# Experts' loop: the first high half of the next up weights moved ahead of ScalarE's evacuation of the block's output

## The reference, cut to what matters

```python
def run_block(args):
    tok, e = args
    xb = hf[jnp.minimum(tok, n_tok - 1)]
    a = xb @ w_gate[e]          # 128x1024 @ 1024x512
    b = xb @ w_up[e]            # 128x1024 @ 1024x512
    return (jax.nn.silu(a) * b) @ w_down[e]   # 128x512 @ 512x1024
```

## Time and profile before

| what | value |
|---|---|
| time, median of 3 runs | 2508.34 us (2498.53 to 2517.55) |
| the profiled execution, its own time | 2503.58 us |
| its span in the trace | 2502.0 us |
| granted TensorE clock over the span | 0.992 |
| 33 blocks of the experts' loop, first evacuation 548.14 to 1146.77 us | 598.63 us, 18.14 us each |
| weights of one expert | 3 x 2048 KB |

### The profile page before, as it was taken

How to read it: one execution, slowest core, us unless ns; L and a number is a source line. 1 busy time by engine, 2 the same in 40 slices (tenths; PEclk the granted TensorE clock), 3 DMA queues, 4 the chain that set the end, 5 groups by cost and what they waited for, 6 DMA issues and landing times. The chain is left out here.

```text
span 2502.0 us, 33881 instructions
## 1 busy us (share of the span) xinstructions
PE 2411.4 (96%) x11969; PEld 1979.1 (79%) x11969; DVE 1910.0 (76%) x2471; ACT 1352.4 (54%) x1914; POOL 589.0 (24%) x492
## 2 busy tenths in 40 slices
PE   7999999999999999999889999999999999999999
PEld 3766678668888888886789999997788888788887
DVE  5876668678988989897877888887776666657786
ACT  3243323257777787775676676676434434444332
POOL 2000354143333232333611110110043333300000
PEclk9999999999999999999999999999999999999999
DMA  7778356589878899998521111113333433587864
GB/s 268 223 240 294 106 197 217 227 309 397 337 272 308 306 403 404 409 398 339 175 68 52 51 51 52 51 39 134 111 110 105 161 139 139 197 305 259 301 253 152
DMA packets 181315, 535.36 MB, mean 214 GB/s; under 512 B 17710, under 2 KB 77714, under 8 KB 167880
## 3 DMA queue, kind: packets, MB, share of 16 engines
q1 hardware_dynamic: 163900, 470.20, 51.5%
q0 software_dynamic: 12592, 45.63, 4.8%
q10 hardware_dynamic: 4700, 17.92, 1.8%
HBM read 443.38 MB, written 90.33 MB: 213 GB/s over the span
## 5 line engine op out<-in xcount | busy, mean ns | idle before, releaser
L1756 PE MATMUL psum<-w_high,block_hT_high 128*128 128x512 f32 x576 | 232.3, 403 | 4.0 <-DVE w_low L1374 2.9
L1374 DVE TENSOR_TENSOR w_low<-first_w_up,w_high 128x2048 fp32r<-128x2048 f32 x72 | 182.8, 2576 | 57.0 <-ACT w_high L1368 57.0
L1758 PE MATMUL psum<-w_high,block_hT_low 128*128 128x512 f32 x576 | 225.3, 391 | 0.0
L1757 PE MATMUL psum<-w_low,block_hT_high 128*128 128x512 f32 x576 | 224.8, 390 | 0.0
L1756 PE MATMUL psum<-w_qkv_high,fox_hT_high 128*128 128x384 f32 (+1 forms) x512 | 181.5, 354 | 10.7 <-DVE w_qkv_low L2603 4.1
L1756 PE MATMUL psum<-w_mlp_out_high,hidden_part_high 128*128 128x512 f32 x448 | 175.6, 392 | 5.1 <-DVE hidden L3992 4.1
L1374 DVE TENSOR_TENSOR w_low<-first_w_gate,w_high 128x2048 fp32r<-128x2048 f32 x74 | 168.6, 2282 | 14.7 <-ACT w_high L1368 14.6
L1758 PE MATMUL psum<-w_mlp_out_high,hidden_part_low 128*128 128x512 f32 x448 | 175.4, 392 | 0.0
L1757 PE MATMUL psum<-w_mlp_out_low,hidden_part_high 128*128 128x512 f32 x448 | 175.2, 391 | 0.0
L1368 ACT ACTIVATE w_high<-first_w_gate 128x2048 fp32r<-128x2048 f32 x74 | 141.3, 1913 | 60.5 <-DMA first_w_gate<-in_w_expert_gate 57.5
L1758 PE MATMUL psum<-w_qkv_high,fox_hT_low 128*128 128x384 f32 (+1 forms) x512 | 173.6, 339 | 0.0
(11 more groups left out here) (523 smaller groups left out, 6742.4 us busy)
## 6 DMA issues: line engine op xcount, KB each, us to landing
first_w_gate<-in_w_expert_gate SPq DMA_DIRECT2D x32, 2048.0 KB, 10.1
first_w_up<-in_w_expert_up SPq DMA_DIRECT2D x32, 2048.0 KB, 10.2
first_w_down<-in_w_expert_down SPq DMA_DIRECT2D x31, 2048.0 KB, 10.3
w_mlp_out_quarters<-in_w_mlp_out SPq DMA_DIRECT2D x78, 512.0 KB, 6.9
hidden_part<-hidden_parts SPq DMA_DIRECT2D x54, 512.0 KB, 4.4
v_aug<-in_w_ada SPq DMA_DIRECT2D x48, 512.0 KB, 5.1
expert_rows<-block_out POOLq DMA_DIRECT2D x34, 512.0 KB, 8.8
v_aug<-in_ada_w SPq DMA_DIRECT2D x32, 512.0 KB, 4.7
```

Source lines behind the costliest of these rows:

```text
L1374: dve.tensor_tensor(wl[:, par, half], raw[kind][:, half], wh[:, par, half].bitcast(F32), ALU.subtract).then_inc(s_wl, 1)
L1756: pe.matmul(out, sh, mh, start=start, stop=False)
L1757: pe.matmul(out, sh, ml, start=False, stop=False)
L1758: return pe.matmul(out, sl, mh, start=False, stop=stop)
```

## The change

In the loop ScalarE's two high halves of the up weights stood together, behind the evacuation. The first half (`(0,)`) now stands ahead of the evacuation of the block before, behind the second high half of gate; the second half (`(1,)`) stays where it was. The first half still waits for its load, and for TensorE to have used the first half of the down weights that lay in that buffer. The last steps of the loop (`left` 1 and 0) have no such half to make. Ahead of the loop the first half for block 1 is made at once. No instruction is added or removed, and no other engine's program is touched.

```diff
                     high_h(1)
+                    split_high(act, "up", 1, up_at(1), 1, (0,))
                     act.wait_ge(t_np, 1)
 
                     def step(n, u, left):
                         if left >= 1:
-                            split_high(act, "up", n + 1, up_at(n + 1), 1 - u)
+                            split_high(act, "up", n + 1, up_at(n + 1), 1 - u, (1,))
...
                             split_high(act, "gate", n + 2, gate_at(n + 2), 1 - u, (1,))
                         if left == 1:
                             split_high(act, "gate", n + 2, down_at(n + 1, 0), 1 - u)
+                        if left >= 2:
+                            split_high(act, "up", n + 2, up_at(n + 2), u, (0,))
                         if left >= 1:
                             act.wait_ge(s_us, down_at(n, left) * 2 + 2)
                             act.wait_ge(s_out[u], n * 8 + (16 - 8 * u))
                             act.activation(ob[:, u, 0:HALF], bank[5], ACT.Copy)
```

## The result

The change makes the kernel slower: 2515.52 us median of 7 runs (2512.42 to 2521.34) against 2506.76 us (2498.53 to 2517.55) for 7 runs of the kernel before, a ratio of 1.0047 with a 95% interval of 1.0028 to 1.0066. That is 12 to 13 us, clear of the scatter and well within 1%. The forecast was 17.8 us more and a range from 2506 to 2541.

A forecast was written before the change was run, and what follows sets the result against it. TensorE and the transfers were taken as nearly the bound together. 29 blocks at 18.8 us and 4 at 17.8 made 616.4 against 598.63 us, so 2508.3 + 17.8 = 2526 us, range 2506 to 2541 (8 in 10).

The forecast's parts named there:

- What bounds the kernel: Experts' loop: TensorE and the transfers are close to being the bound together, blocks taking 18.14 us on average.
- The chain over the evacuation: Experts' loop: end of down, evacuation, high half, low half, up products, down products, repeating every 18.01 us.
- the transfers keep their 18.1: In the 20 or so blocks at 1.00 DMA share, the transfers set 18.1 us even if the gap is used.
- The gain: Start of up products: an earlier low half saves TensorE 0.2 us, a TensorE-paced block taking 17.8 us.
- The wait that moves with the half: ScalarE before the evacuation: waits 2.5 us for the up load, evacuation then 1.8 us behind the landing.
- GpSimd and VectorE: Up low halves: the first holds GpSimd's product, which holds the second; up loads land every 8.79 us plus load time.
- a loop of 7.2 + L: Landing-to-landing loop without the hold, L being up-load time from issue to landing: claimed shorter than TensorE's block, costing nothing.
- The size: 33 blocks: 29 x 18.8 + 4 x 17.8 = 616.4 us against 598.63, 17.8 us more, up loads assumed 10.0 us.
- The signs named for the profile: Loop profile: ScalarE idle 2 to 3 us per block, GpSimd's product about 3.5 us, TensorE waiting about 1 us more.
- A gap that is used after all: Rival: up loads under 9.0 us let the half use ScalarE's gap, 3 us faster, 2505; chance 0.1 with another case.
- The rival in which nothing is seen: Rival: up loads of 9.4 to 9.6 us, a loss of 0 to 6 us, 2511; chance 0.15.
- the one with a longer load: Rival: up loads of 10.3 us and more as the store falls into them, 29 us more, 2538; chance 0.25.

The follow-up runs named there:

- both_ahead: Against the change: both high halves of the next up weights stand ahead of the evacuation; ratio to the kernel before 0.9928, 2485.15 us, again 0.9946, 2488.52 us.
- no_up_load_before: The kernel before without the 29 up loads of the loop, so products use wrong weights; ratio to the kernel before 0.9973.
- gpsimd_later: The changed kernel with GpSimd's product also waiting until VectorE has made the second low half of the next up weights; ratio to the kernel before 0.9940.
- small_product_change: The changed kernel with GpSimd's product on 8 columns of 1024, the other columns left unscaled; ratio to the kernel before 0.9955.
- change_again: The changed kernel as it is, measured once more beside the kernel before; ratio 1.0051.

## Why the prediction was right, and where it was not

**What bounds the kernel.** The chain over the evacuation was read rightly: without up loads the old order takes its 18.01 us everywhere, and the floor of TensorE is 17.77, where the prediction had 17.8. The other half of that step failed. The prediction took the 404 GB/s and 1.00 of the DMA engines in the earlier trace rows for a bound of their own, "the transfers keep their 18.1". both_ahead moves the same bytes at 415 GB/s with a share of 1.01 and takes 17.77 us in exactly those blocks. So the blocks of 18.1 to 18.8 us of before were not the limit of the transfers. They vanish when the up loads are taken out (no_up_load_before) and when VectorE is done with up earlier (both_ahead; gpsimd_later has 17.5 to 18.0 in them), so the loads had a part in them, as links of a loop. Which link was the slow one stands in the trace of before. A block of it takes 18.01 us plus what GpSimd's product takes over 2.40, to 0.04 us in all 33; the product is longer where it is issued while the second low half of gate still runs; and that half is late where the gate load is late (ScalarE waits 1.7 to 3.1 us for it ahead of each block over 18.1). For the block of the earlier trace rows (18.78 us, product 3.17) the wait and its end at TensorE are:

```profile
597.03 1.92 ACT L1368 ACTIVATE w_high<-first_w_gate 128x2048 fp32r<-128x2048 f32 x1 [3.14 <-DMA first_w_gate<-in_w_expert_gate]
```

```profile
609.07 0.50 PE L1756 MATMUL psum<-w_high,block_hT_high 128*128 128x512 f32 x1 [0.68 <-DVE w_low L1374]
```

That a stretch shows 1.00 is what a loop with three loads under way looks like too.

**The gain.** Sized at 0.2 us a block; the pair without up loads shows 0.22 (18.02 to 17.80), the pair with halved loads 0.21 and the pair with the small product 0.18. The change as made never gets it.

**The wait that moves with the half.** Right in place, cause and size. The landing was 0.13 us ahead of the old evacuation in the typical block, and ScalarE now waits 2.75 us in 28 blocks; 2 to 3 were forecast.

**GpSimd and VectorE.** Right, to 0.03 us in each step of the block shown, and gpsimd_later and small_product_change show that the slowdown needs it: take it out, leave the wait, and the slowdown is gone. The halved loads show that it needs the load in the loop as well. The Trainium skill has the same rule ("SBUF — State Buffer", Who interferes with whom), and the traces agree with it: 3.54 and 3.93 us in the change for 2.40 and 2.28 alone, one held until the other is through. One reading here was wrong: a loop of 7.2 + L is not shorter than TensorE's block "for any L of the rows". With the longest of the earlier trace rows, 11.1, it is 18.3 us; it is shorter only up to an L of 10.6. In small_product_change, with 7.28 and an L of 10.7, such a loop still takes 18.0 us, and the period is 17.91.

**The size.** The sum was 29 x 18.8 + 4 x 17.8 = 616.4 us for the 33 blocks, and the profile has 617.43. From a landing to the next issue the change takes 8.92 us in all but two blocks, 0.13 more than the sum's 8.79, of which 0.11 is the time from the landing to ScalarE's start, which the sum left out; L is 10.0 as a median but 9.84 as a mean, and the two errors cancel. That L was 10.0 was an assumption that came out, not a result of the sum: the same load has 10.5 to 10.7 in the faster kernels. The single blocks are not as forecast: where the weights are there early, as with a repeated expert, the evacuation falls back towards TensorE's end and the distance is 16.4 to 17.2 us, not 17.8, and the one behind it is up to 21.2. Over the loop this evens out, and the mean is the one that was worked out. In the time of the kernel the loss is 12 to 13 us, not 17.8. Counted from the first evacuation to the last one of all, the two profiles of the change lose 17 and 15 us (633.49 and 631.09 against 616.25 us), and the intervals of the ratios reach to 16.5 and 16.8. So the term is about 5 us too large against the middle of the ratios, and the runs don't show whether that is scatter or is given back behind the loop. Against this one profile of before, ten of the twelve kernels measured come out 1 to 6 us faster by their ratio than by their loop, so part of it may lie in that profile.

**The signs named for the profile.** ScalarE idle in front of the first high half, L1470 at 3.54, hardly a wait for TensorE in front of the evacuation (3.6 us in 4 blocks), TensorE waiting at the second half of up (17.4 us in 25 blocks, 0.7 each, where about 1 was named), all came. "The loads of gate would show no waits to speak of" did not: 30.1 us are left of 55 before, while the wait for down loads grew to 24.8 from 9.5. No run tests what these cost in the changed order.

**The rivals.** A gap that is used after all needed L under 9.0; it was 10.0, with single loads of 7.7 to 8.9. The rival in which nothing is seen needed 9.4 to 9.6, and the one with a longer load 10.3 and more: the store that falls into the load did not lengthen its median.

## What to carry to other kernels

Before an instruction is moved into an idle gap of its engine, look up when each of its inputs arrives: a gap in front of a wait may be as long as the time that the input is still under way, and then everything behind the instruction on that engine waits for the input as well. Then look at what the later instructions release, and on whose instructions those fall: here a product of GpSimd that had met an idle VectorE came to lie between two halves that a load was waiting for, and moving one half more, or the product, or asking for the load earlier, turned +0.5% into -0.5 to -0.7%. And don't take a DMA share of 1.00 for a bound when the transfers are links of a loop; it is one only if no other order moves more.

## What the runs showed of the hardware

- VectorE's subtraction with both inputs in SBUF and GpSimd's product exclude each other. In the change GpSimd's 2.40 us become up to 4.10 (once 6.53 in change_again, behind two halves) and VectorE's 2.28 for one half up to 4.50. A product that waits ends 2.24 to 2.28 us behind the end of the half that held it (734.37 to 736.64 in the block above), and a half that waits ends 2.14 to 2.16 behind the product, each a little less than its own time.
- One core moved 415 GB/s over 100 us (both_ahead and gpsimd_later, 900 to 1000 us), six sevenths of it the three loads of 2048 KB in each block, with TensorE busy all the time and VectorE for 93 of the 100 us.
- An up or down load of 2048 KB took 7.5 to 12.8 us from issue to landing in the experts' loops of these kernels, with what else was in the queues. A change of order that left the bytes alone moved the median of the up loads from 10.2 to 10.0 (the change) and 10.6 us (both_ahead), and without the up loads the down loads took 7.9 (no_up_load_before, median) instead of 10.3.
